# Down chunks 0 to 2 by seven block products, weight sums made in DRAM, activation sums on GpSimd

## The reference

```python
def sq_relu_mlp(h, w_up, w_down):
    u = jnp.einsum('btd,df->btf', h, w_up)
    return jnp.einsum('btf,fd->btd', jnp.square(jax.nn.relu(u)), w_down)
...
        h = h + sq_relu_mlp(rms_norm_2(h, mlp_norm_g[layer]), mlp_w_up[layer], mlp_w_down[layer])
```

## Time and profile before

| | us |
|---|---|
| median of 3 runs | 1832.25 (1831.91 to 1832.4) |
| the profiled execution | 1835.86 |
| its span on the core | 1834.0 |
| PE busy | 1789.8 (98%) |
| DVE busy | 1150.3 (63%) |
| ACT busy | 866.9 (47%) |
| GpSimd busy | 450.9 (25%) |
| mean DMA rate | 81 GB/s |

### The profile page before, as it was taken

The page is one execution under the profiler, slowest core; times in us unless marked ns, Lnnn a source line. Parts: engine busy times, 40 slices in busy tenths (PEclk is TensorE's granted clock), DMA queues, the critical chain, the costliest instruction groups (busy, mean ns, idle before and its releaser), DMA issues.

```text
span 1834.0 us, 26208 instructions
## 1 busy us (share of the span) xinstructions
PE 1789.8 (98%) x10340; PEld 1460.4 (80%) x10340; DVE 1150.3 (63%) x1861; ACT 866.9 (47%) x1409; POOL 450.9 (25%) x451
## 2 busy tenths in 40 slices
PE   7999999999999999999999999999999999999997
PEld 6877777775678757677879898988888787989896
DVE  5355556575546688854578575765677657858574
ACT  5236665455435465564345252633445434435253
POOL 0035551101311235560140000005678214000000
PEclk9999999999999999999999999999999999999999
DMA  5321111231013411111232322222222123232322
GB/s 177 101 78 49 47 47 58 80 101 50 24 47 100 133 60 34 36 36 58 80 122 86 115 93 104 93 97 83 84 88 76 46 81 127 81 115 92 106 91 80
DMA packets 44521, 149.20 MB, mean 81 GB/s; under 512 B 6000, under 2 KB 6384, under 8 KB 44400
## 3 DMA queue, kind: packets, MB, share of 16 engines
q1 hardware_dynamic: 44400, 147.53, 24.1%
HBM read 139.64 MB, written 2.10 MB: 77 GB/s over the span
## 4 chain that ended last, share of the span: by engine, by line
PE 85%; DVE 6%; ACT 4%; POOL 2%; issue 2%; DMA 1%; POOLq 0%; SPq 0%; DVEq 0%; ACTq 0%
PE BANK L301 18%; PE BANK L303 17%; PE BANK L302 17%; PE BANK L2405 4%; PE BANK L2404 4%; PE BANK L2402 4%; PE BANK L955 3%; PE BANK L688 2%; PE BANK L1739 1%; PE BANK L1720 1%; DMA WRAW<-in_wc 1%; DVE WL L278 1%; PE BANK L1696 1%; PE BANK L1012 1%; PE BANK L2710 1%
## 5 line engine op out<-in xcount | busy, mean ns | idle before, releaser
L269 ACT ACTIVATE WH<-WRAW 128x1024 fp32r<-128x1024 f32 (+1 forms) x214 | 223.0, 1044 | 340.8 <-PE BANK L303 306.0
L278 DVE TENSOR_TENSOR WL<-WRAW,WH 128x1024 fp32r<-128x1024 f32 (+1 forms) x201 | 256.3, 1276 | 138.8 <-ACT WH L269 138.6
L301 PE MATMUL BANK<-HH,WH 128*128 128x512 f32 x664 | 273.1, 411 | 12.1 <-DVE WL L278 9.8
L303 PE MATMUL BANK<-HL,WH 128*128 128x512 f32 x664 | 260.2, 392 | 0.0
L302 PE MATMUL BANK<-HH,WL 128*128 128x512 f32 x664 | 259.9, 391 | 0.0
L301 PE MATMUL BANK<-HIDH,WH 128*128 128x512 f32 (+1 forms) x520 | 201.2, 387 | 1.6 <-issue 1.5
L302 PE MATMUL BANK<-HIDH,WL 128*128 128x512 f32 (+1 forms) x520 | 200.7, 386 | 0.0
L303 PE MATMUL BANK<-HIDL,WH 128*128 128x512 f32 (+1 forms) x520 | 200.7, 386 | 0.0
L2405 PE MATMUL BANK<-HP,G 128*128 128x256 f32 x672 | 190.2, 283 | 0.0
L2404 PE MATMUL BANK<-HP,G 128*128 128x256 f32 x672 | 190.2, 283 | 0.0
L2402 PE MATMUL BANK<-HP,G 128*128 128x256 f32 x672 | 190.1, 283 | 0.0
(11 more groups left out here) (446 smaller groups left out, 3694.2 us busy)
## 6 DMA issues: line engine op xcount, KB each, us to landing
WRAW<-in_w SPq DMA_DIRECT2D x77, 512.0 KB, 3.5
WRAW<-in_wd SPq DMA_DIRECT2D x64, 512.0 KB, 3.5
RAW<-in_wf SPq DMA_DIRECT2D x32, 512.0 KB, 3.6
WRAW<-in_wu SPq DMA_DIRECT2D x16, 512.0 KB, 3.5
TMP<-in_wf SPq DMA_DIRECT2D x16, 512.0 KB, 3.5
WRAW<-in_w0o SPq DMA_DIRECT2D x8, 512.0 KB, 3.5
WRAW<-in_w1o SPq DMA_DIRECT2D x8, 512.0 KB, 3.4
WRAW<-in_wc SPq DMA_DIRECT2D x8, 512.0 KB, 3.5
```

The lines of the kernel that those rows point to most:

```text
L269: e.activation(WH[b % NS][:, 0:n], WRAW[b % NR][:, 0:n], ACT.Copy).then_inc(*inc("s_high", ("high", b)))
L278: e.tensor_tensor(WL[b % NS][:, 0:n], WRAW[b % NR][:, 0:n], WH[b % NS][:, 0:n].bitcast(F32), ALU.subtract).then_inc(*inc("s_low_pool" if p ...
L301: e.matmul(dst, ah, bh, start=first and i == 0, stop=False)
L303: made = e.matmul(dst, ah, bl, start=False, stop=last and i == len(sets) - 1)
```

## The change

- Down chunks 0 to 2 are made by the seven products too. `FAST` now lists 48 steps a layer: down 0, up 1, down 1, up 2, down 2, up 3. Only up chunk 0 and down chunk 3 stay direct. In a down chunk the first two pairs run interleaved by halves (pair 0, pair 1, pair 0, pair 1), so that the planes made last are needed last; for the same reason their last steps take the seven products in the order `LATE`.
- The hidden activations therefore need seven planes for each of four pairs. There is one buffer for it, `D` (it is `TMP`, 8 x 256 wide). Up chunk 0 runs its tiles as 0, 4, 1, 5, 2, 6, 3, 7; DVE evacuates a pair of tiles into `D`, ACT squares it there, GpSimd makes the sums in three operations (`hid_mix`), ACT and DVE split all seven into `HID[p]` (`hid_high`, `hid_low`). The next pair is written to `D` only when that is over. In up chunks 1 and 2 the same follows `Q`: relu, square into `D`, mix, split. `STAGE` is now one buffer, and planes 2 and 3 of the input go through `D` as well, in steps 2 to 6.
- Results of a down pair are joined in `Q` and added to `X` by GpSimd (`add_pool`), no longer by DVE from PSUM.
- The sums of weight quarters aren't made on DVE. SP copies 96 pieces of 512 KB into a DRAM tensor `sums` (`sums_first`, one or two behind each block's load in the first layers), and GpSimd issues 48 adding transfers of 1 MB on it (`sums_add`), spread over its work in all layers but the last. A step's load is now two transfers, 384 KB of weights and 512 KB of sums.
- `RAW`'s third buffer now lies over `WRAW`, and the three slots of `WH`, `WL` lie under two of the `G` buffers, so the first steps wait for the last tiles of up chunk 0, and the blocks of down chunk 3 wait for the last steps.

```diff
-FAST = [(c, pair, half) for c in range(1, 4) for pair in range(4) for half in range(2)]
+UP_ORDER = (0, 4, 1, 5, 2, 6, 3, 7)
+FAST = [(kind, c, pair, half) for kind, c in (("dn", 0), ("up", 1), ("dn", 1), ("up", 2), ("dn", 2), ("up", 3))
+        for pair, half in (((0, 0), (1, 0), (0, 1), (1, 1)) if kind == "dn" else ((0, 0), (0, 1), (1, 0), (1, 1))) +
+        ((2, 0), (2, 1), (3, 0), (3, 1))]
...
+        def sums_add(e, w, n):
+            for i in range(sums_add.done, min(sums_add.done + n, 4 * SUMS)):
+                g, step = 2 * (i // 8) + i % 2, i % 8 // 2
+                w.wait_ge(*dma(f"s_first{g}", 8))
+                if step:
+                    w.wait_ge(*dma(f"s_sums{g}", step))
...
+                e.dma_start(A["sums"][g][:, 2048 * dst:2048 * dst + 2048], src, accum_op=ALU.add,
+                            max_dma_last_dim=4096).then_inc(*dma(f"s_sums{g}"))
...
+            e.dma_start(raw_part(s, 1, 3), A[f"wf{L}"][s]).then_inc(*dma(f"s_raw{s % 3}"))
+            w.wait_ge(*dma(f"s_sums{g}", 4))
+            e.dma_start(RAW[s % 3][:, 4:8, :], sums_of(g)[:, :, s % 8, :]).then_inc(*dma(f"s_raw{s % 3}"))
...
+        def hid_mix(e, w, L, c, p):
+            w.wait_ge(*at("hid square", L, c, p))
+            turn_pool(e, w, D, "hid", L, c, p)
...
+        def add_pool(e, w, L, c, p):
+            w.wait_ge(*at("joined", L, "dn", c, p, 3))
...
+            e.tensor_tensor(X[:, p + 4, :], X[:, p + 4, :], flat(Q[:, 0:2, :]), ALU.add).then_inc(*inc("s_x_added"))
+            e.tensor_tensor(X[:, p, :], X[:, p, :], flat(Q[:, 2:4, :]), ALU.add).then_inc(
+                *inc("s_x_added", ("x added", L, c, p)))
...
         def mlp_vector(e, w, L):
...
                 w.wait_ge(*at("tile", ("up", L, 0), m))
-                if m > 3:
-                    w.wait_ge(*at("hid lo", L, 0, m - 4))
-                e.scalar_tensor_tensor(out=TMP[:, m % 4, :], in0=banks[("up", L, 0), m], scalar=0.0, in1=RS[:, :],
+                if i > 1:
+                    w.wait_ge(*at("hid lo", L, 0, i // 2 - 1))
+                at_d = 6 if m < 4 else 4
+                e.scalar_tensor_tensor(out=flat(D[:, at_d:at_d + 2, :]), in0=banks[("up", L, 0), m], scalar=0.0, in1=RS[:, :],
                                        op0=ALU.max, op1=ALU.mult).then_inc(*inc("s_evac", ("evac", ("up", L, 0), m)))
...
         def mlp_gpsimd(e, w, L):
...
+            hid_mix(e, w, L, 0, 0)
+            plane_mix(e, w, L, 0, STAGE)
+            hid_mix(e, w, L, 0, 1)
+            plane_mix(e, w, L, 1, STAGE)
+            hid_mix(e, w, L, 0, 2)
```

519 lines of the change are left out of this document (319 added, 200 removed).

## The result

The changed kernel is slower, and by twice what was forecast: **1911.7 us** in the median of 4 runs (1909.2 to 1917.1) against 1832.1 for the kernel before on the same chip, a ratio of 1.044 (95% interval 1.042 to 1.046). The forecast was 1872.3, with a range that ended at 1896. The sign was right, and so was the main mechanism inside the feed-forward parts; +80 us stand where +40 were forecast. The profiled execution took 1917.1 us, its span is 1915.0.

A forecast was written before the change was run, and what follows sets the result against it. TensorE was taken as the bound: per layer -10.8 + 19.0 + 2.5 + 2 x 4.5 = +19.7, two layers +39.4, sums +0.6, so +40 us on 1832.25. Forecast 1872.3 us, range 1840 to 1896.

The forecast's parts named there:

- PE's own work: Feed-forward layer: 296.3 us of TensorE chunks become 285.5 with seven products, a gain of 10.8 a layer.
- start of the part, to step 0: Start of each feed-forward layer: serial chain through D plus GpSimd/DVE collisions delays the steps by 19.0 us, undisturbed 12.5.
- down chunk 0, and up chunk 1 behind it: Down chunk 0: a stall at step 6 from DVE and GpSimd load, 2.5 us taken between 0 and 5.
- up 1 to down 1, up 2 to down 2: Up chunk into down chunk, twice a layer: the pair's chain delays PE 4.5 us each, between 0 and 6.3.
- sums in the DRAM, once: Copies on SP and adding transfers on GpSimd: 0.6 us taken, GpSimd's bounds nothing and 13; an issue up to 2.4 hidden.
- The mean of the first mix operation: Expected sign in the profile after: GpSimd's first mix operation averages over 2 us.
- the 3.9 that I laid in: Up chunk into down chunk: a mix taking 3.9 us on GpSimd, which gives a delay of 3.2 us.
- some 64: Expected sign: a layer's first product some 64 us after the start of the first up tile, 44.7 before the change.
- held by its adding transfers until they land: Rival, chance 0.10: GpSimd held until each transfer lands; first layer pays 53 us, so 1925, or 1885 at 3.5 us.
- 5 us ahead of the parts: Sign of being wrong: the layers ahead of the feed-forward grow by more than 5 us.
- collisions hardly occur: Rival, chance 0.16: GpSimd and DVE slip past each other, 1835 to 1838 us, up to 1856 with half the collisions.
- "faster": Rival, chance 0.10: the start's chain is shorter, 1820 to 1830 us; below a start stall of 10.8 a layer gains.

The follow-up runs named there:

- e12: Changed kernel with GpSimd's mixing in buffer D on 8 elements of each block instead of 256 (output wrong): 1868.7 us.
- e18: Changed kernel with one edit, the mixing of the hidden planes on VectorE instead of GpSimd: 1885.6 us.
- e6: Changed kernel with a buffer for each pair of up tiles in turn, low parts made behind the next pair's first evacuation: 1901.3 us.
- e9: e6 plus up chunk 0's last two evacuations ahead of pair 2's low part, and plane 1's high part ahead of the sixth square: 1890.1 us.
- e4b: Kernel before with one added TensorE wait in each feed-forward part, at down chunk 0's fifth tile (14.8 us each): 1866.6 us.
- e5: Changed kernel with products of no use in the two long TensorE waits of each feed-forward part: 1914.2 us.
- e20: e9 with adding transfers spread (4 KB pieces), hidden planes mixed on VectorE, and the late edits: 1851.0 us.
- the late edits: Two edits, in e20 (1851.0 us): VectorE's fast low parts ahead of planes 2 and 3, TensorE's bank wait ahead of that bank's first product.

## Why the prediction was half right

The terms of one feed-forward part, forecast and measured (first part; chunk lengths of the windows against 40.32, the start against 44.70):

| term | forecast | measured |
|---|---|---|
| PE's own work | -10.8 | -10.8 (chunks of 40.32 us do occur) |
| start of the part, to step 0 | +19.0 | +16.7 |
| down chunk 0, and up chunk 1 behind it | +2.5, 0 | +8.0, +2.2 |
| up 1 to down 1, up 2 to down 2 | +4.5, +4.5 | +4.6, +5.2 |
| down chunk 3 | 0 | +1.2 |
| sum | +19.7 | +27.1 |
| sums in the DRAM, once | +0.6 | 16 in the adding transfers, 2.7 in the copies (medians) |

By the medians +79.6 us stand against +40. The copies and adding transfers have 18.5 of it, for 0.6; the two parts with what follows them 53.5 by the table, for 39.4. The rest is the 3.7 us ahead of the parts that stay without any sums, and the 3.8 by which the profiled execution of before lies above its median.

- **PE's work and the transitions were right.** The bracket of 0 to 6.3 with 4.5 taken gave 4.6 and 5.2, and e12 and e18 show the cause that was named: without GpSimd's mix these waits are gone, and with them 9.8 us a part. The chain was priced from the earlier trace rows, and that sufficed. The mean of the first mix operation, which should have exceeded 2 us, is 1.66; the collisions lie on the other two (1.42 and 1.26 for 0.74 undisturbed). The mix as a whole takes 4.33, more than the 3.9 that I laid in.
- **The start was right in size and too simple in cause.** 61.5 us from the first up tile to step 0 stand against "some 64": PE waits 3.2 us ahead of the eighth up tile and 10.8 ahead of step 0, and the other 2.7 are its own work at a lower clock between the two (0.67 from 950 to 955). I said that D serves one pair at a time. e6 took that away and won 6.8 us of 16.7, e9 by order alone 5.3 more. The laying out of durations was good because it followed the in-order queues, and D was only one of their waits.
- **Down chunk 0 was the mis-sized term of the part**: 2.5, with bounds 0 and 5, against 10.2 with the chunk behind it. 5.1 are waits (1.24, and 3.90 ahead of up chunk 1, ended by VectorE's weight subtraction), and 4.9 are PE's clock, which fell in the long wait ahead of step 0 and again in the 3.9. The sum had no term for the clock at all. e4b gives its price: half of the time that it stays low behind a wait, 4.6 to 6.0 us here. e5 shows that this price isn't always paid: without the low clock PE waited 2.4 us for VectorE instead. So what the 2.5 had wrong is in the main how late VectorE is. I had laid in 16 us for the eight adds on GpSimd; they take 3.01 and 2.07 us in the mean, 20.3 a chunk, and VectorE's weight subtraction takes 2.24 for 2.02.
- **The sums were the failed step.** I wrote that GpSimd's issue has no row and took 0.6 from SP's 0.33 us, against bounds of 0 and 13; they cost 18.5. An issue takes 1.16 us, within the 2.4 that I had found hidden; but a second one behind it stands still for some 4 us, until the first has landed, and the low parts of the first layer, with 1.4 us to spare, wait with it. The rival "held by its adding transfers until they land" had the place, the victim and the event; what it had wrong is that the first transfer holds nobody, only the next one issued before it has landed is held back, and that this goes by the number of pieces. The price, 16, lies between its 13 and 53 us. I had named 5 us ahead of the parts as the sign that I was wrong, and it is there.
- **Down chunk 3 had no term.** Its matmuls are the same 192 and nothing waits, but they start 0.233 us apart where they were 0.227 apart: 1.2 us. No run says why.
- **The rivals.** That collisions hardly occur, and "faster", are excluded by the mix's 4.33 us. "Faster" was to decide at a start stall of 10.8 us: e9 and e20 reach 4.7, and yet none is faster, because down chunk 0 and up chunk 1 lose 5.2 and 1.6 more in e20 (8.0 and 1.6 in e9), which the rival had at nothing, and e9 has GpSimd's mixes and the stops besides.

Open: the 3.7 us ahead of the parts that are left with no sums; the matmuls of down chunk 3; and the 3.9 us ahead of up chunk 1, which neither buffers nor VectorE's mixing of the hidden planes moved, which the late edits cut to 2.5 and the small mixes to 1.8.

## What to carry to other kernels

Where an engine's operations are new to a trace, take the price of a run of them and not of one: one adding transfer cost GpSimd 1.2 us, one issued before it had landed 5.3. What a hold costs is read from what stands behind it: the adding transfers with 58.8 us of stops cost 16 us, and spread, with 48.7 us of stops elsewhere, 3 (1898.7 against the 1895.9 without them). Before work moves to an idle engine, ask what each result then waits for: GpSimd was 25% busy and had room, but its 4.3 us stood in a chain that another engine closes in 1.5. And when a chain of several engines feeds one that was never idle, the order in their queues can be worth as much as a buffer.
